# One wide product for both halves of a mixing matrix, with VectorE adding the two parts

## The reference

```python
def chunk_sgu(h, w_in, v_norm, w_s, b_s, w_out):
    z = jax.nn.gelu(h @ w_in)
    u, v = jnp.split(z, 2, axis=-1)
    v = rmsnorm(v, v_norm)
    ...
    vc = vp.reshape(B, Lp // CHUNK, CHUNK, SGU_GROUPS, SGU_GROUP_DIM)
    ws = w_s * jnp.tril(jnp.ones((CHUNK, CHUNK), dtype=w_s.dtype))
    mixed = jnp.einsum('gts,bcsgd->bctgd', ws, vc) + jnp.transpose(b_s)[:, :, None]
    mixed = mixed.reshape(B, Lp, D_SGU)[:, :L]
    return (u * mixed) @ w_out, v
```

## Time and profile before

| | |
|---|---|
| time, median of 3 runs | 764.1 us (761.37 to 764.32) |
| profiled execution | 762.99 us, its span 761.2 us |
| PE busy | 737.3 us (97%) |
| DVE, ACT, POOL busy | 300.5, 403.7, 539.1 us |
| granted TensorE clock, mean | 0.994 |

### The profile page before, as it was taken

The page is one execution under the profiler, slowest core; times in us unless marked ns, Lnnn a source line. Parts: engine busy times, 40 slices in busy tenths (PEclk is TensorE's granted clock), DMA queues, the critical chain, the costliest instruction groups (busy, mean ns, idle before and its releaser), DMA issues.

```text
span 761.2 us, 16830 instructions
## 1 busy us (share of the span) xinstructions
PE 737.3 (97%) x6315; PEld 717.0 (94%) x6315; DVE 300.5 (39%) x742; ACT 403.7 (53%) x708; POOL 539.1 (71%) x255
## 2 busy tenths in 40 slices
PE   6999999999999999999998899999999999999995
PEld 5999999999999999999986788889999999999995
DVE  5435855423233232222685555662232332331102
ACT  5867554556444444556554465554464444454542
POOL 7976766978888888899765112218869888878891
PEclk9999999999999999999999999999999999999998
DMA  8554453656777755556564689715546555555641
GB/s 311 189 181 139 142 164 116 221 179 202 239 235 234 235 178 184 196 191 206 182 249 128 178 264 311 286 47 166 184 136 210 191 180 178 178 181 191 198 163 58
DMA packets 44919, 144.65 MB, mean 190 GB/s; under 512 B 5602, under 2 KB 6882, under 8 KB 44610
## 3 DMA queue, kind: packets, MB, share of 16 engines
q1 hardware_dynamic: 44722, 143.53, 57.9%
q0 software_dynamic: 144, 0.40, 0.1%
HBM read 142.42 MB, written 1.48 MB: 189 GB/s over the span
## 4 chain that ended last, share of the span: by engine, by line
PE 78%; DVE 3%; ACT 1%; issue 1%; DVEq 0%; ACTq 0%
PE ps L1281 24%; PE ps L1282 24%; PE ps L1283 24%; PE ps L1596 1%; PE ps L1620 1%; PE ps L1543 1%; PE ps L1600 0%; PE ps L1567 0%; ACT whi L465 0%; DVE olo L802 0%; PE ps L1307 0%; DVE ps L1083 0%; PE ps L1475 0%; PE ps L1677 0%; PE ps L1610 0%
## 5 line engine op out<-in xcount | busy, mean ns | idle before, releaser
L394 POOL TENSOR_TENSOR wlo<-raw,whi 128x1024 fp32r<-128x1024 f32 x222 | 529.2, 2404 | 202.5 <-ACT whi L465 202.1
L1281 PE MATMUL ps<-xhi,whi 128*128 128x264 f32 x1052 | 304.1, 289 | 0.9 <-DVE olo L802 0.9
L1282 PE MATMUL ps<-xlo,whi 128*128 128x264 f32 x1052 | 298.8, 284 | 0.0
L1283 PE MATMUL ps<-xhi,wlo 128*128 128x264 f32 x1052 | 298.6, 284 | 0.0
L465 ACT ACTIVATE whi<-raw 128x1024 fp32r<-128x1024 f32 x222 | 233.8, 1054 | 54.9 <-PE ps L1283 54.0
L1281 PEld LDWEIGHTS ps<-xhi,whi 128*128 128x128 f32 x1052 | 198.9, 189 | 1.9 <-DVE olo L802 1.1
L1282 PEld LDWEIGHTS ps<-xlo,whi 128*128 128x128 f32 x1052 | 199.1, 189 | 0.4
L1283 PEld LDWEIGHTS ps<-xhi,wlo 128*128 128x128 f32 x1052 | 198.1, 188 | 0.0
L1281 PE MATMUL ps<-ahi,whi 128*128 128x264 f32 x352 | 100.0, 284 | 0.0
L1283 PE MATMUL ps<-ahi,wlo 128*128 128x264 f32 x352 | 99.9, 284 | 0.0
L1282 PE MATMUL ps<-alo,whi 128*128 128x264 f32 x352 | 99.9, 284 | 0.0
(11 more groups left out here) (252 smaller groups left out, 1109.1 us busy)
## 6 DMA issues: line engine op xcount, KB each, us to landing
raw<-w_stream SPq DMA_DIRECT2D x222, 512.0 KB, 3.4
pg<-pages SPq DMA_DIRECT2D x64, 288.0 KB, 3.6
pg<-w_ukT SPq DMA_DIRECT2D x1, 2048.0 KB, 8.3
pg<-w_uv SPq DMA_DIRECT2D x1, 2048.0 KB, 9.8
h<-xT SPq DMA_DIRECT2D x4, 264.0 KB, 4.7
y_out<-h SPq DMA_DIRECT2D x4, 264.0 KB, 2.2
raw<-w_stream SPq DMA_DIRECT2D x2, 256.0 KB, 3.4
wsraw<-wsT SPq DMA_DIRECT2D x1, 512.0 KB, 7.3
```

Source lines behind the costliest of these rows:

```text
L394: pool.tensor_tensor(wlo[:, c % RING, :], raw[:, c % RING, :], whi[:, c % RING, :].bitcast(F32), ALU.subtract).then_inc(lo_ready, 1)
L1281: pe.matmul(out, whi_, mhi, start=start, stop=False)
L1282: pe.matmul(out, whi_, mlo, start=False, stop=False)
L1283: return pe.matmul(out, wlo_, mhi, start=False, stop=stop)
```

## The change

The high and low part of a mixing matrix become neighbours in one tile, `wsboth`. With `vthi` as stationary operand one matmul of 256 columns multiplies both; `vtlo` multiplies the high part alone and adds to the first half. A token chunk takes two matmuls in place of three, and the bank then holds two parts that VectorE has to add: a new instruction scales the second part and adds the bias into an SBUF row (`sq`), the old one scales the first part and adds that row, and the copy of the sample columns comes after both, since its columns hold a part of the second product until then.

```diff
-            wshi = sb("wshi", [P, 2, GROUPS, P], F32R, a)
-            wslo = sb("wslo", [P, 2, GROUPS, P], F32R, a)
+            wsboth = sb("wsboth", [P, 2, GROUPS, 2, P], F32R, a)
...
                 wait(dve, mix_done, u_ + 1, i, 4)
+                mixed, below = (ps[:, bank, x * NP_:(x + 1) * NP_].rearrange("p (a t) -> p a t", a=2) for x in range(2))
+                low = sq[:, u_ % 2, 0:NP_].rearrange("p (a t) -> p a t", a=2)
+                dve.scalar_tensor_tensor(out=low, in0=below, scalar=gv[:, at, :],
+                                         in1=bsb[:, i * 2 + u_ // 2, :].unsqueeze(1).broadcast_to([P, 2, P]),
+                                         op0=ALU.mult, op1=ALU.add).then_inc(mixl_done, 1)
+                wait(dve, mixl_done, u_ + 1, i, 4)
+                dve.scalar_tensor_tensor(out=mixed, in0=mixed, scalar=gv[:, at, :], in1=low, op0=ALU.mult,
+                                         op1=ALU.add).then_inc(mixr_done, 1)
+                wait(dve, mixr_done, u_ + 1, i, 4)
                 dve.tensor_copy(ps[:, bank, NP_:T], mbs[:, at, :]).then_inc(mbc_done, 1)
-                mixed = ps[:, bank, 0:NP_].rearrange("p (a t) -> p a t", a=2)
-                dve.scalar_tensor_tensor(out=mixed, in0=mixed, scalar=gv[:, at, :],
-                                         in1=bsb[:, i * 2 + u_ // 2, :].unsqueeze(1).broadcast_to([P, 2, P]),
-                                         op0=ALU.mult, op1=ALU.add).then_inc(mixr_done, 1)
                 wait(dve, mbc_done, u_ + 1, i, 4)
-                wait(dve, mixr_done, u_ + 1, i, 4)
                 wait(dve, gelu_done, KS + u_ + 1, i, 4)
...
                 for c in range(2):
-                    last = passes(ps[:, 4 + u_ % 4, c * P:c * P + P], vthi[:, at, c, :], vtlo[:, at, c, :],
-                                  wshi[:, c, g, :], wslo[:, c, g, :], True, True)
+                    both = ps[:, 4 + u_ % 4, :].rearrange("p (h a t) -> p h a t", h=2, a=2)[:, :, c, :]
+                    pe.matmul(both, vthi[:, at, c, :], wsboth[:, c, g], start=True, stop=False)
+                    last = pe.matmul(both[:, 0], vtlo[:, at, c, :], wsboth[:, c, g, 0], start=False, stop=True)
                 last.then_inc(mix_done, 1)
```

More of the change, by code:

```diff
@@ L251, in build @@
             sem, ("gelu_done", "wshi_done", "wslo_done", "vsr_done", "vs_done", "vt_done", "vthi_done", "vtlo_done"))
-        mix_done, mixr_done, mbs_done, gt_done, ghi_done, glo_done = map(
-            sem, ("mix_done", "mixr_done", "mbs_done", "gt_done", "ghi_done", "glo_done"))
+        mix_done, mixl_done, mixr_done, mbs_done, gt_done, ghi_done, glo_done = map(
+            sem, ("mix_done", "mixl_done", "mixr_done", "mbs_done", "gt_done", "ghi_done", "glo_done"))
         mbc_done, gsc_done, usc_done = map(sem, ("mbc_done", "gsc_done", "usc_done"))
@@ L575, in mixing_high @@
                 for c in range(2):
-                    act.activation(wshi[:, c, 4 * half:4 * half + 4], wsraw[:, 4 * half:4 * half + 4], ACT.Copy,
+                    act.activation(wsboth[:, c, 4 * half:4 * half + 4, 0], wsraw[:, 4 * half:4 * half + 4], ACT.Copy,
                                    scale=Rv[:, NS + c:NS + c + 1]).then_inc(wshi_done, 1)
@@ L913, in mixing_low @@
                     dve.wait_ge(wshi_done, 2 * half + c + 1)
-                    dve.scalar_tensor_tensor(out=wslo[:, c, g], in0=wsraw[:, g], scalar=Rv[:, NS + c:NS + c + 1],
-                                             in1=wshi[:, c, g].bitcast(F32), op0=ALU.mult,
+                    dve.scalar_tensor_tensor(out=wsboth[:, c, g, 1], in0=wsraw[:, g], scalar=Rv[:, NS + c:NS + c + 1],
+                                             in1=wsboth[:, c, g, 0].bitcast(F32), op0=ALU.mult,
                                              op1=ALU.subtract).then_inc(wslo_done, 1)
```

## The result

| | kernel before | changed kernel |
|---|---|---|
| time, median of 8 runs | 763.77 us (761.37 to 767.81) | 767.06 us (766.08 to 767.85) |
| ratio | | 1.0047, 95% interval 1.0028 to 1.0066 |
| profiled execution, its span | 762.99, 761.2 us | 767.66, 764.4 us |
| PE, DVE busy | 737.3, 300.5 us | 735.4, 303.0 us |
| granted clock, mean | 0.994 | 0.992 |

The change makes the kernel 0.47% slower; the forecast was 767.3 us. In four of its eight executions 2.2 to 3.3 us lie around the span (3.3 in the profiled one), in the other four 1.8 to 1.9; no run shows what that is.

What follows compares the result with a forecast made beforehand. TensorE, busy in 97% of the span, bounds the kernel on average, but VectorE ends the changed stage. A 3.0 us later restart and 1.35 us of clock loss add 4.3 us to 762.99, giving 767.3 us; range 763.0 to 770.5.

Steps and rivals of the forecast that it cites:

- TensorE's saving: Mixing matmuls on TensorE: a unit falls from 3.57 to 3.36 us, 3.4 us less over 16 units.
- The straight unit: VectorE's unit in straight code grows from 2.22 to 2.85 us, with 0.63 us more in the gate.
- Unit 2's start: VectorE starts unit 2 late, at 86.34 us, after low-matrix instructions wait for GpSimd; claimed to stay unchanged.
- The rival with another order at the lock: Second L914 goes ahead of GpSimd's slab, VectorE 2.1 us earlier: 765.2 us with the clock's loss, 763.9 without; chance 0.12.
- The loop unit: VectorE's unit in the loop takes 3.38 us against TensorE's 3.36, so VectorE never catches up.
- 0.46 us to the next unit: Last piece of VectorE's loop unit, from `glo` to the next unit's start, taken as 0.46 us.
- The tail: Units 12 to 15 on VectorE: 7.22 us grows to 9.74 us, from the first copy or gate to the last `glo`.
- the wait: TensorE goes on at 129.7 us instead of 126.69 at the stage's end, 3.0 us later.
- The clock: TensorE's idle stretches before 129.7 us lower its clock; 3 us at the low level cost 1.35 us.
- my upper bound: Upper bound of the clock's loss: two such low-clock stretches, costing 2.7 us.
- the rival without a fall: Clock stays at 2.4 GHz since blocks trickle in; 3.0 us delay alone, 765.9 us; chance 0.16.
- The sum: Delay and clock loss together add 4.3 us to the profiled 762.99, giving 767.3 us.

Runs made afterwards that it cites:

- experiment 1: Changed kernel's wide product with VectorE's old gate, copy first; the bank's second part is left out of the result. Ratio 0.9959 to the kernel before.
- experiment 2: Changed kernel with the wide product undone, three matmuls of 128 columns per token chunk, VectorE's add kept. Ratio 1.0059 to the kernel before, 766.9 us.
- experiment 6: Changed kernel with both instructions of the low mixing matrices' second half moved to where GpSimd is idle. Ratio 1.0008 to the kernel before.
- experiment 5: Changed kernel without VectorE's low parts of the mixing matrices of groups 4 to 7, early memsets instead. Ratio 1.0024 to the kernel before.
- experiment 8: Kernel before with the wide product and the add in units 12 to 15 alone, old form in units 0 to 11. Ratio 1.0045.
- experiment 4: Changed kernel with 36 filler matmuls (8, 14, 14) ahead of TensorE's waits for blocks 13, 14, 15. Ratio 1.0022 to the kernel before.
- experiment 7: Kernel before with only the move of the low mixing matrices' second half to where GpSimd is idle. Ratio 0.9997.
- experiment 3: Changed kernel with 57 filler matmuls (9, 16, 16, 16) ahead of TensorE's blocks 12 to 15. Ratio 1.0047 to the kernel before.
- experiment 9: Changed kernel with the low-matrix instructions moved, new form in units 0 to 11, old form in 12 to 15. Ratio 0.9967 to the kernel before.
- experiment 10: Changed kernel with no move, new form only in loop units 4 to 11, old form elsewhere. Ratio 0.9963 to the kernel before.

## Why the prediction was right, step by step

- **TensorE's saving.** Forecast 0.21 us per unit, 3.36 for a unit. Measured (116.05 - 75.65)/12 = 3.367. Right, and shown to be hidden by experiments 1 and 2.
- **The straight unit.** Forecast 2.85, measured 2.83 (1.24 for the gate against 1.27).
- **Unit 2's start.** Forecast unchanged at 86.34; measured 86.72 with a start 0.37 later. The second L913 again takes 2.88 us. The rival with another order at the lock did not come.
- **The loop unit.** Forecast 3.38, measured 3.25. The gate's 1.42 is the mean of the eight, and L951 to `glo` is 1.11 as taken. Mis-sized is "0.46 to the next unit": it stood on one row; here seven of eight have 0.35 and one 0.62 (mean 0.38), and L837's full 0.43 was never needed. Over eight units this is 1.0 us too much.
- **The tail.** Forecast 9.74, measured 9.62. Together with the loop, the wait came to 1.78 instead of 3.0 us. The pieces of idleness are three (blocks 13 to 15), not four, and 4.8 us in all, not 6.9: TensorE had done its small pieces at 122.8, not at 121.7.
- **The clock.** Forecast 1.35, from 3 us at the low level, after the one example in the trace; measured 2.45, with 5.45 us of work at 1.2 GHz (128.84 to 134.29). By the three stretches above the clock was low for 0.32 x 2 x 4 + 4 + 0.04 x 2 x 4 = 6.9 us, twice the 3.4 of the earlier trace rows, which is the case of my upper bound, 2.7. The mechanism was right and its size 1.1 too small. The size is not a fixed one: with the same tail on VectorE, the profiles lost 2.45 us (changed kernel), 1.54 (experiment 2), 1.47 (experiment 6) and nothing (experiments 5 and 8), and TensorE's last two waits were the same within 0.01 us in 5, 6 and 8. So the rival without a fall did come in two of five profiles. For the changed kernel itself the loss is not that of one execution: all eight have a mean clock of 0.988 to 0.992, the twelve of experiment 4 have 0.990 to 0.997.
- **The sum** was 4.3, and the stage gives 4.23. That is luck: the wait was 1.2 too large and the clock 1.1 too small. It is luck once more that 767.3 lies 0.2 us from the measured median. The whole time rose by 3.3 (medians) and the span by 3.2, not by 4.3. The forecast started from 762.99, which is 0.8 under the median of the kernel before, and some of the changed kernel's executions have more time around the span. I had also missed that the kernel before loses the clock in the attention in some executions and not in others, so that a fall here can be one less there; one pair of profiles shows that, and experiment 6's has both falls.

Left open: how often in the mean over executions each fall happens, and what decides it after equal waits. The profiles show single executions, and experiment 8's shows that a fall saved in the stage can come back later.

## What to carry to other kernels

Before trading TensorE time for an instruction in another engine's chain, look for the place where TensorE waits for that chain: there the whole added chain counts, and in all other places only what exceeds the slack. An engine that has once come late needs slack per step to get back; a longer step of nearly the bound's own period keeps it late to the end of the stage. A change can be good in the loop and bad in its tail, and can then be made in the one alone.

## What the runs showed of the hardware beyond that

- The kernel's scatter goes with the clock. Of the 23 executions of the kernel before that stood beside experiments 4 and 8, those with a mean clock of 0.996 or 0.997 took 761.2 to 761.7 us, those with 0.994 took 762.3 to 763.8 (one 765.3), and those with 0.991 to 0.993 took 765.0 to 766.0.
- The same idle stretch of 2.55 to 2.60 us lies ahead of the attention's 32 matmuls in all twelve profiles. In six (the kernel before and experiments 4 to 8) the clock was low behind it and the 32 matmuls took 2.99 to 3.47 us; in the other six (the changed kernel and experiments 1, 2, 3, 9 and 10) they took 1.91.
- A unit with the old gate took 1.83 to 1.85 us in the tails of experiments 1, 9 and 10 instead of 1.89, although it has the same instructions; what differs is that the two self-waits ahead of the multiply by `u` have changed places. No run tests that alone.
- L913 with both inputs in SBUF took 0.7 us beside an idle GpSimd and 2.88 beside a busy one. The new add with one input in PSUM took 0.47 to 0.48 us in all 16 units, in 12 of them with GpSimd at work for all or part of that time.
